# A diffusion-backbone step on one core: modulation blocks packed into shared PSUM banks by zero-padded conditions, one rotation per run

## The reference, cut to what matters

```python
cond_p, cond_s = jax.nn.silu(c_ctx), jax.nn.silu(c)
for i in range(2):
    mod_p = jnp.split(cond_p @ ada_w[i] + ada_b[i], 6, axis=-1)      # ada_w[i]: 1024 x 6144
    mod_s = jnp.split((cond_s @ ada_w[i] + ada_b[i])[:, None, :], 6, axis=-1)
    hs = xs * (1 + mod_s[1]) + mod_s[0]                              # into the mixer (same for xp with mod_p)
    xs = post_norm(xs, mod_s[2] * mixer(hs), ...)
    hs = xs * (1 + mod_s[4]) + mod_s[3]                              # into the ConvFFN
    xs = post_norm(xs, mod_s[5] * conv_ffn(hs), ...)
```

## Time and profile before

| | before |
|---|---|
| median of 3 runs | 1912.0 us (1909.44 to 1913.46) |
| the profiled execution's own time | 1910.59 us |
| its span | 1908.8 us |
| mean granted TensorE clock | 0.967 of full |
| TensorE busy | 1785.9 us (94%), 11636 matmul records |
| DVE busy | 1016.6 us (53%) |
| ACT busy | 697.9 us (37%) |
| GpSimd busy | 668.8 us (35%) |
| DMA | 165.08 MB, mean 86 GB/s |

### The profile page before, as it was taken

One profiled execution on the slowest core, in us unless ns is written; L12 is line 12 of the kernel. 1 busy time (PEld: TensorE's weight loads), 2 busy tenths in 40 slices (PEclk: granted clock), 3 DMA queues, 4 the chain that ended last, 5 costly groups with the idle time before them and its releaser, 6 DMA issues.

```text
span 1908.8 us, 30276 instructions
## 1 busy us (share of the span) xinstructions
PE 1785.9 (94%) x11636; PEld 1665.6 (87%) x11636; DVE 1016.6 (53%) x1542; ACT 697.9 (37%) x1074; POOL 668.8 (35%) x292
## 2 busy tenths in 40 slices
PE   7999999769899999999997999998889999999996
PEld 3688888659899999999996899998779999999996
DVE  2476766545665622656517645534547771277723
ACT  3245554432522311222216445545253231132323
POOL 3212122226543333323455222222565343333444
PEclk8999999789899999999998899999889999999998
DMA  9611111002244321444221111110112222122221
GB/s 385 226 45 51 41 50 51 28 12 73 93 169 171 124 76 56 165 176 154 91 68 32 46 62 56 51 50 28 55 45 77 72 84 76 55 77 77 79 76 55
DMA packets 50072, 165.08 MB, mean 86 GB/s; under 512 B 5696, under 2 KB 11328, under 8 KB 49984
## 3 DMA queue, kind: packets, MB, share of 16 engines
q1 hardware_dynamic: 43648, 159.68, 23.7%
q10 hardware_dynamic: 6336, 4.20, 0.7%
HBM read 159.12 MB, written 4.74 MB: 86 GB/s over the span
## 4 chain that ended last, share of the span: by engine, by line
PE 86%; DVE 6%; ACT 3%; issue 2%; DVEq 1%; DMA 1%; SPq 0%; POOL 0%; ACTq 0%; POOLq 0%
PE pj L577 71%; PE mO L987 2%; PE psS L726 2%; PE psO L768 2%; PE pfrow L616 1%; PE psT L742 1%; PE psT L751 1%; PE prow L600 1%; DVE pr L1825 1%; DMA awr<-in_w_ada 1%; PE mS L943 1%; PE pfmod L623 1%; PE psT L776 1%; PE pmod L607 0%; PE mT L1012 0%
## 5 line engine op out<-in xcount | busy, mean ns | idle before, releaser
L457 POOL TENSOR_TENSOR wlo<-wraw,whi 128x1024 fp32r<-128x1024 f32 (+1 forms) x130 | 350.7, 2698 | 851.2 <-ACT whi L1119 851.2
L577 PE MATMUL pj<-Hh,whi 128*128 128x322 f32 x2400 | 579.0, 323 | 46.3 <-issue 18.8
L577 PE MATMUL pj<-Hl,whi 128*128 128x322 f32 x2400 | 560.1, 315 | 0.0
L577 PE MATMUL pj<-Hh,wlo 128*128 128x322 f32 x2400 | 556.1, 313 | 0.0
L577 PEld LDWEIGHTS pj<-Hh,whi 128*128 128x128 f32 x2400 | 407.3, 192 | 77.4 <-issue 51.7
L577 PEld LDWEIGHTS pj<-Hl,whi 128*128 128x128 f32 x2400 | 412.7, 192 | 0.0
L577 PEld LDWEIGHTS pj<-Hh,wlo 128*128 128x128 f32 x2400 | 412.2, 192 | 0.0
L1119 ACT CAST whi<-wraw 128x1024 fp32r<-128x1024 f32 (+1 forms) x182 | 201.8, 1109 | 345.7 <-PE pj L577 298.9
L1684 DVE SCALAR_TENSOR_TENSOR X<-pj,mods,X 128x129 f32<-128x129 f32 (+1 forms) x144 | 54.6, 436 | 284.1 <-PE pj L577 284.0
L1741 DVE SCALAR_TENSOR_TENSOR fcv<-fus,vec,fcv 128x644 f32<-128x644 f32 x88 | 168.9, 1920 | 15.0 <-issue 15.0
L577 PE MATMUL pj<-Gh,whi 128*128 128x322 f32 x704 | 162.2, 312 | 0.0
(11 more groups left out here) (313 smaller groups left out, 2129.2 us busy)
## 6 DMA issues: line engine op xcount, KB each, us to landing
wraw<-in_w_up SPq DMA_DIRECT2D x88, 512.0 KB, 3.5
fwr<-in_w_ada SPq DMA_DIRECT2D x56, 512.0 KB, 5.9
wraw<-in_w_dn SPq DMA_DIRECT2D x32, 704.0 KB, 4.1
awr<-in_w_ada SPq DMA_DIRECT2D x40, 512.0 KB, 10.5
wraw<-in_w_qkv SPq DMA_DIRECT2D x24, 512.0 KB, 3.5
wraw<-in_w_mlin SPq DMA_DIRECT2D x24, 512.0 KB, 3.5
wraw<-in_w_wo SPq DMA_DIRECT2D x8, 512.0 KB, 3.4
wraw<-in_w_mlout SPq DMA_DIRECT2D x8, 512.0 KB, 3.5
```

Of the source, the lines that this page charges most:

```text
L457: nc.gpsimd.tensor_tensor(wlo[k][:, 0:width], wraw[k][:, 0:width], whi[k][:, 0:width].bitcast(F32), ALU.subtract).then_inc(w_lo, 1)
L577: last = mm(out[:, c, 0:HALF], w, x[:, j, c * HALF:(c + 1) * HALF], start=(j == 0 and n == 0), stop=(j == n_k - 1 and n == 2))
```

## The change

The stationary operand becomes 32 columns wide: a buffer of zeros (`conda`, `condf`, 128 x 8 x 62) holds the two condition columns at column 30, and block b of a run takes the 32 columns from 30 - 2b on, so its two conditions come to columns 2b and 2b + 1 and all others are zero. All blocks of a run accumulate into one bank, each into its own two rows of every column group. The runs are blocks 0 to 3, blocks 4 to 9, and the 7 blocks of each half of the FFN. After a run, DVE copies the bank once (128 rows) and TensorE turns it once, with a `pick` of up to 14 columns. So the 24 copies and turns become 4, and 8 matmul records a turn stay as they are; the blocks keep their 16 records. The up steps that stood in a loop with blocks and turns are written out. The bank needs no clearing. The order of the rest, the DMAs and their waits stay.

```diff
 FS = 4
-ROWS = 98
+RUN = 7
+PAD = 30
...
             fwr = [sb(f"fwr{k}", [P, 2, 512], F32, s) for k in range(FS)]
-            frow = sb("frow", [ROWS, 512], F32, s)
+            frow = sb("frow", [P, 512], F32, s)
+            condf = sb("condf", [P, KT, PAD + 32], F32, s)
         with ExitStack() as s:
...
             awr += [sb(f"awr{k}", [P, 2, 512], F32, s) for k in range(5, AS)]
-            arow = [sb(f"arow{k}", [ROWS, 512], F32, s) for k in range(2)]
+            arow = sb("arow", [P, 512], F32, s)
+            conda = sb("conda", [P, KT, PAD + 32], F32, s)
         with ExitStack() as s:
...
             pspare = ps("pspare", [P, 2, 512], s)
-            pmod = ps("pmod", [P, 4 * NB, 2], s)
-            pspare1 = ps("pspare1", [P, 512], s)
-            prow = [ps(f"prow{k}", [ROWS, 512], s) for k in range(2)]
+            pmod = [ps(f"pmod{k}", [P, 4, 2 * RUN], s) for k in range(2)][::-1]
+            prow = [ps(f"prow{k}", [P, 512], s) for k in range(2)]
         with ExitStack() as s:
             pspare2 = ps("pspare2", [P, 2, 512], s)
-            pfrow = ps("pfrow", [ROWS, 512], s)
-            pfmod = ps("pfmod", [P, 4 * NF, 2], s)
+            pfrow = ps("pfrow", [P, 512], s)
+            pfmod = ps("pfmod", [P, 4, 2 * RUN], s)
         with ExitStack() as s:
...
-            def ada_block(n):
-                if n > 1:
-                    pe.wait_ge(row_copied, n - 1)
+            def block(b, n, out, conds, bufs, landed, used, at):
                 for kp in range(4):
-                    u = 4 * n + kp
-                    pe.wait_ge(aw_landed[u % AS], 16 * (u // AS + 1))
+                    u = at + kp
+                    pe.wait_ge(landed[u % len(bufs)], 16 * (u // len(bufs) + 1))
                     for r in range(2):
                         g = 32 * ((2 * kp + r) % 4)
-                        last = mm(prow[n % 2][g:g + 2, :], cond[:, 2 * kp + r, :], awr[u % AS][:, r, :], start=(kp < 2), stop=(kp >= 2))
-                    last.then_inc(aw_used, 1)
-            def ada_turn(n):
-                pe.wait_ge(row_copied, n + 1)
+                        last = mm(out[g:g + 32, :], conds[:, 2 * kp + r, PAD - 2 * b:PAD - 2 * b + 32], bufs[u % len(bufs)][:, r, :],
+                                  start=(b == 0 and kp < 2), stop=(b == n - 1 and kp >= 2))
+                    last.then_inc(used, 1)
+            def ada_block(n):
+                k = 0 if n < 4 else 1
+                block(n - 4 * k, 6 if k else 4, prow[k], conda, awr, aw_landed, aw_used, 4 * n)
+            def ada_turn(k):
+                pe.wait_ge(row_copied, k + 1)
+                w = 12 if k else 8
                 for q in range(4):
-                    last = mm(pmod[:, 4 * n + q, :], arow[n % 2][:, q * P:(q + 1) * P], pick[0:ROWS, :], start=True, stop=True)
+                    last = mm(pmod[k][:, q, 0:w], arow[:, q * P:(q + 1) * P], pick[:, 0:w], start=True, stop=True)
                 last.then_inc(row_turned, 1)
...
             def ffn_block(n):
-                for kp in range(4):
-                    pe.wait_ge(fw_landed[kp], 16 * (n + 1))
-                    for r in range(2):
-                        g = 32 * ((2 * kp + r) % 4)
-                        last = mm(pfrow[g:g + 2, :], cond[:, 2 * kp + r, :], fwr[kp][:, r, :], start=(kp < 2), stop=(kp >= 2))
-                    last.then_inc(fw_used, 1)
-            def ffn_turn(n):
-                pe.wait_ge(frow_copied, n + 1)
+                block(n % RUN, RUN, pfrow, condf, fwr, fw_landed, fw_used, 4 * n)
+            def ffn_turn(half):
+                pe.wait_ge(frow_copied, half + 1)
                 for q in range(4):
-                    last = mm(pfmod[:, bass.ds(4 * n + q, 1), :].rearrange("p a b -> p (a b)"), frow[:, q * P:(q + 1) * P], pick[0:ROWS, :],
-                              start=True, stop=True)
+                    last = mm(pfmod[:, q, :], frow[:, q * P:(q + 1) * P], pick[:, :], start=True, stop=True)
                 last.then_inc(frow_turned, 1)
...
                     else:
-                        up(2)
                         if half == 0:
-                            pe.wait_ge(rows_clear, 2)
-                        ffn_block(7 * half)
-                        with pe.Fori(3, 9) as i:
+                            pe.wait_ge(cond_padded, 2)
+                        for i in range(2, 2 + RUN):
                             up(i)
-                            ffn_turn(i + (7 * half - 3))
-                            ffn_block(i + (7 * half - 2))
+                            ffn_block(RUN * half + i - 2)
                         up(9)
-                        ffn_turn(7 * half + 6)
+                        ffn_turn(half)
                         up(10)
...
             pe.wait_ge(ones_ready, 1)
-            pe.wait_ge(cond_ready, 1)
-            pe.wait_ge(rows_clear, 1)
-            ada_block(0)
-            ada_block(1)
+            pe.wait_ge(cond_padded, 1)
+            for n in range(4):
+                ada_block(n)
             ada_turn(0)
-            ada_block(2)
-            ada_turn(1)
-            ada_block(3)
-            ada_turn(2)
-            ada_turn(3)
...
             ada_block(5)
-            ada_turn(4)
             qkv(2, [4, 5, 6, 7])
             ada_block(6)
-            ada_turn(5)
             qkv(3, [0, 1])
             ada_block(7)
-            ada_turn(6)
             qkv(3, [2, 3])
             ada_block(8)
-            ada_turn(7)
             qkv(3, [4, 5])
             ada_block(9)
-            ada_turn(8)
             qkv(3, [6])
-            ada_turn(9)
+            ada_turn(1)
             for h in range(DA_HEADS):
...
-            def add_bias(pm, t0, t1, base=0):
-                b = vec[:, V_ADAB + t0:V_ADAB + t1]
-                last = tt(mods[:, t0:t1, :], pm[:, t0 - base:t1 - base, :], b[:, :, None].to_broadcast([P, t1 - t0, 2]), ALU.add)
-                if t1 == 4 * NB:
+            def add_bias(pm, t0, n):
+                pm4 = pm[:, :, 0:2 * n].rearrange("p q (b m) -> p b q m", m=2)
+                m4 = mods[:, t0:t0 + 4 * n, :].rearrange("p (b q) m -> p b q m", q=4)
+                b4 = vec[:, V_ADAB + t0:V_ADAB + t0 + 4 * n].rearrange("p (b q) -> p b q", q=4)
+                last = tt(m4, pm4, b4[:, :, :, None].to_broadcast([P, n, 4, 2]), ALU.add)
+                if t0 == 16:
                     last.then_inc(mods_ready, 1)
...
-            def copy_rows(n):
-                dve.wait_ge(aw_used, 4 * (n + 1))
-                if n > 1:
-                    dve.wait_ge(row_turned, n - 1)
-                nc.vector.tensor_copy(arow[n % 2][:, :], prow[n % 2][:, :]).then_inc(row_copied, 1)
-            def copy_block(n):
-                dve.wait_ge(fw_used, 4 * n + 4)
+            def copy_rows(k):
+                dve.wait_ge(aw_used, 4 * NB if k else 16)
+                if k:
+                    dve.wait_ge(row_turned, 1)
+                nc.vector.tensor_copy(arow[:, :], prow[k][:, :]).then_inc(row_copied, 1)
+            def copy_block(half):
+                dve.wait_ge(fw_used, 4 * RUN * (half + 1))
                 nc.vector.tensor_copy(frow[:, :], pfrow[:, :]).then_inc(frow_copied, 1)
+            def pad_cond(t):
+                nc.vector.memset(t[:, :, :], 0.0)
+                dve.drain()
+                dve.wait_ge(cond_ready, 1)
+                nc.vector.tensor_copy(t[:, :, PAD:PAD + 2], cond[:, :, :]).then_inc(cond_padded, 1)
...
                         if half == 0:
-                            nc.vector.memset(pfrow[:, :], 0.0).then_inc(rows_clear, 1)
-                        loop(dve, 2, body)
-                        with dve.Fori(2, 9) as i:
-                            body(i)
-                            copy_block(i + (7 * half - 2))
+                            pad_cond(condf)
+                        loop(dve, 9, body)
+                        copy_block(half)
                         with dve.Fori(9, GH) as i:
                             body(i)
-                        dve.wait_ge(frow_turned, 7 * half + 7)
-                        add_bias(pfmod, 4 * (NB + 7 * half), 4 * (NB + 7 * half + 7), 4 * NB)
+                        dve.wait_ge(frow_turned, half + 1)
+                        add_bias(pfmod, 4 * (NB + RUN * half), RUN)
                     if half == 0:
...
             dve.wait_ge(const_in, 16)
-            tt(pick[:, :], ident[:, 0:2], ident[:, 32:34], ALU.add)
-            for k in range(2):
-                nc.vector.memset(prow[k][:, :], 0.0)
-            dve.drain()
-            tt(pick[:, :], pick[:, :], ident[:, 64:66], ALU.add)
-            dve.drain()
-            tt(pick[:, :], pick[:, :], ident[:, 96:98], ALU.add).then_inc(rows_clear, 1)
+            pad_cond(conda)
+            tt(pick[:, :], ident[:, 0:2 * RUN], ident[:, 32:32 + 2 * RUN], ALU.add)
+            for g in (64, 96):
+                dve.drain()
+                tt(pick[:, :], pick[:, :], ident[:, g:g + 2 * RUN], ALU.add)
             for k in range(2):
```

(20 more changed lines are left out.)

## The result

Six runs of the changed kernel took 1897.41 to 1900.46 us, median **1899.0 us**; six of the kernel before, run beside them, 1909.44 to 1913.83, median 1911.3. The ratio is 0.9936 [0.9926, 0.9947], so 12.3 us less. The forecast was 1898.5 us with a range of 1893 to 1905.5. The two profiled executions lie 13.2 us apart, a span of 1895.6 after 1908.8; the forecast's sum was 13.0.

The account below looks back on a forecast made before the run. TensorE, busy 94% of the 1908.8 us span, was taken to bound the kernel. Terms -9.7 - 4.5 + 0.7 - 0.2 + 0.6 + 0.1 = -13.0 us led to a forecast of 1898.5 us, range 1893 to 1905.5.

Parts of the forecast that it names:

- Turns in the FFN: In the FFN 14 turns become 2; 12 removed turns at 0.81 us each give -9.7 us.
- Turns in the prologue: In the attention prologue six turns (blocks 4 to 9) become one; five at 0.9 us each give -4.5 us.
- The wait for unit 39: In block 9 of the prologue TensorE waits for its last modulation unit: +0.7 us, bounds 0 and 1.6.
- The low bound: Unit 39 moves with its own issue, two turns earlier, landing at 78.7, so TensorE's wait is 0.
- Before 31 us: In the first four blocks, bound by data, three of four turns go: -0.2 us, bounds 0 and -1.
- Padded loads: In all 24 blocks 32-column loads take 25 ns more, one per block in the open: +0.6 us, bounds 0 and 9.6.
- The kept turns: The four turns that stay stream 8 to 14 columns instead of 2: +0.1 us.
- a us or two: Attention heads and mLSTM, untouched by the edits, should keep their length within this; giving the gain back makes the forecast wrong.
- (a): Rival: padded loads in the blocks are not hidden, 0.4 us more per block, 9.6 us in all, 1907.5 us; chance 0.07.
- (b): Rival: in the prologue blocks wait for their data units and the 4.5 us are not gained, 1902.3 us; chance 0.09.
- (c): Rival: the FFN's 14 written-out up steps each lose 1 us to instruction supply, 1912.5 us; chance 0.04.
- (d): Rival: in the 24 blocks the four column groups stop running side by side, about 2018 or 1940 us; chance 0.04.

Follow-up runs that it names:

- empty turns: Changed kernel with 12 turns put back on TensorE alone at their old FFN places, no wait or copy, result unused: 1909.2 us, ratio 0.9987 to the kernel before.
- padding alone: Kernel before with the stationary of all 24 blocks padded to 32 columns and all 24 turns kept: 1912.3 us, ratio 1.0009.
- keep-warm version: Changed kernel plus unused dense matmuls, 3 after the prologue's first turn and 8 ahead of each FFN: 1896.4 us, ratio 0.9918 to the kernel before.

## Why the prediction was right, step by step

- **Turns in the FFN, -9.7 us.** Measured -9.4 in the two halves. 12 x 0.81 = 9.7 less the padded loads of 14 blocks (14 x 0.022 = 0.3) is 9.4: the term is right, and so are the two terms together. It needs the turn with its entry and exit (0.81), from the difference of two periods, not its own 0.79. The empty turns cost 0.80 each in the same loop.
- **Turns in the prologue, -4.5.** Measured -4.31 with six padded blocks in it, so -4.44 for five turns, 0.89 each; 0.9 was taken between 0.79 and 0.98. The block's exit is paid in part by the QKV matmuls that now follow it (12 records in 1.98 us for 1.88).
- **The wait for unit 39, +0.7.** This is the step that failed, by its size. The forecast let the train of units move by 0.9 us, with the release of block 6's units. But unit 39 has an issue of its own, which block 7 releases, and that came at 70.83 for 73.24, 2.4 us sooner; its transit was 7.0 us for 7.3. It landed 2.7 us sooner, at 77.8 for 80.5. The low bound (it moves with its own issue) was the true one. With block 9 one step earlier the wait appeared, 1.34 us.
- **Before 31 us, -0.2.** Block 4 started 0.69 us earlier. The first projection gained 1.14. Of that, 0.47 was not foreseen: the loads behind the last unit started at 28.42 for 28.89. Some 0.6 is the clock, which the forecast had named as a cost only: in the profiled execution it came back to 1.00 at 26.4 us for 30.0, so the last records of block 3 were done 1.1 us after their loads for 1.7. The turns that went gave less than 0.1: the copy and one turn (0.70 and 1.07 us) now stand where two turns took 1.97. From there to block 4, 0.45 us of it went again. The kernel before had block 4 at 52.41 and 55.22, the changed one at 51.72 and 51.75, so this term is known no better than to 3 us.
- **Padded loads, +0.6.** Measured 0.5: a load of 110 ns for an estimate of 105, and one of sixteen in the open. The rule of the Trainium skill that stands in the prediction (page "TensorE: Matmul & The Clock Gate", Part 3, "The mechanism": a load overlaps matmuls in flight only where the row groups differ) would, by that sentence alone, have blocks of about 2.2 us; they take 1.85, and all loads take all 128 rows. So here the rule does not hold, and the measurement decides. That the different column groups are the reason is not shown: in an up step all 96 records use all columns, and their loads of 0.19 us each make 18 us, but the step takes 14.49.
- **The kept turns, +0.1.** 0.80 and 0.81 us for 0.79: 0.01 to 0.02 each, under 0.1 in all.
- **What no term held.** +1.44 us in the heads, most of it from one step that fell into a stretch of half clock. The forecast allowed untouched stages "a us or two", and this was of that size. That the sum came out at -13.2 for -13.0 is luck: the missing wait (-0.7), the start (-0.5) and 0.3 us between and behind the halves made up for it. The medians differ by 12.3 us. In the second profile of the changed kernel the heads went beyond the "us or two": from the scores to the norm's first record the chain took 389.1 us, where the first profile had 386.5 and the two of before 385.1 and 385.8. Over all profiles it is 385.1 to 385.9 in the four whose prologue is not packed, and 385.3 to 389.1 in the eight where it is, on average 1.3 us more. So part of the prologue's gain may as a rule be given back there; two of the eight lost nothing, and no run isolates the cause.

**The rivals.** (a), loads not hidden, asked for blocks of 2.2 us and fell with the padding alone. (b), data setting the prologue's pace: no block waits, and the gain is 4.3 of 4.5 us; but it lies 0.5 us away for block 9, and the keep-warm version shows a weight tile due next. (c), written-out up steps: 14.49 us each, and with the empty turns between them the old period returned but for the padding. (d), column groups no longer side by side: 16 records of 592 ns in 1.85 us say that they still are.

## What to carry to other kernels

Price a removed step by the difference of two periods of the same loop, not by its own duration; where the chain is one engine without a gap, such differences came within 0.1 us of what each of the two places gave. For data that is wanted earlier, shift each transfer by its own release and leave its transit as it is. And take gains under some 3 us from repeated runs or from a stretch that repeats between profiles (here from the first norm on), for what comes before it moves by that much from one profile of this kernel to the next, with the clock's course.

## What the runs showed of the hardware

- The granted clock takes another course from one execution to the next of the same program: half clock for 20.48 us or for two times 6.83 at the start of the kernel before; in the changed one for 3.41 or 6.83 us from about 23 us on, 6.83 more from about 33 us, and none or 3.41 us at 84 us. Work on the chain that fell into such a stretch took 1.2 to 1.3 us longer (12 matmuls in 3.34 us for 2.02, four records of the RMS sums in 2.50 for 1.34).
- The clock can be kept up by matmuls that nobody reads: with eight of 512 columns behind two norms it stayed at 1.00 where it had been at 0.68 on average, and the kernel ran 1.9 us shorter from there. The five runs with them behind three norms took 1891.5 to 1897.7 us, the five of the changed kernel beside them 1899.1 to 1900.3.
- A 32-column f32 stationary loads in 105 to 110 ns, one of 2 columns in 80 to 84, and a block with 16 such loads grew from 1.83 to 1.85 us.
- A unit of 512 KB, issued while the DMA engines were busy throughout (99% from 70.4 to 79.8 us in the kernel before), landed 6.97 to 7.3 us after its own issue, in three kernels, though the issue moved by 2.4 us.
